# Two-layer encoder trunk: eight slots for split weights in the FFN, its last step by token block, block 0 turned at another place, first loads in another order

## What is computed

```python
for l in range(DEPTH):                      # DEPTH = 2, ALPHA = 4**0.25
    x = layer_norm(ALPHA * x + 0.5 * swiglu(x, ffn1_w13[l], ffn1_w2[l]), ...)
    h = x @ w_in[l]                         # pool channels | q | kv | rope key
    y_mix = concat([pool_mixer(...), mla_mixer(...)]) @ w_out[l]
    x = layer_norm(ALPHA * x + y_mix, ...)
    y_mem = memory_cross_attention(x, mem, mem_wq[l], mem_wkv[l], mem_wo[l])
    x = layer_norm(ALPHA * x + y_mem, ...)
    x = layer_norm(ALPHA * x + 0.5 * swiglu(x, ffn2_w13[l], ffn2_w2[l]), ...)

def swiglu(x, w13, w2):                     # d_ff = 2816
    gate, up = jnp.split(x @ w13, 2, axis=-1)
    return (jax.nn.silu(gate) * up) @ w2
```

## Time and profile before

| | us |
|---|---|
| median of 3 runs | 1175.89 (1175.66 to 1176.28) |
| the profiled execution, its time | 1177.25 |
| the profiled execution, its span | 1175.5 |
| PE busy in the span | 1123.4 |
| DVE busy | 717.6 |
| ACT busy | 511.7 |
| mean granted clock of TensorE | 0.987 |

### The profile page before, as it was taken

One profiled execution on the slowest core, in us unless ns is written; L12 is line 12 of the kernel. 1 busy time (PEld: TensorE's weight loads), 2 busy tenths in 40 slices (PEclk: granted clock), 3 DMA queues, 4 the chain that ended last, 5 costly groups with the idle time before them and its releaser, 6 DMA issues.

```text
span 1175.5 us, 16505 instructions
## 1 busy us (share of the span) xinstructions
PE 1123.4 (96%) x6020; PEld 968.4 (82%) x6020; DVE 717.6 (61%) x856; ACT 511.7 (44%) x670; POOL 106.1 (9%) x116
## 2 busy tenths in 40 slices
PE   5999999999999999999999999999999998999996
PEld 4888888899899888888888888879888986888884
DVE  3655555878766765555585555567768757555555
ACT  3544444346355254444444444434553524444440
POOL 5800000150100100000010000001401000000001
PEclk9999999999999999999999999999899998999998
DMA  8655666434482486666556665544335527665650
GB/s 257 208 185 181 194 192 196 140 117 157 126 268 93 126 267 189 186 182 194 162 183 211 194 188 188 181 141 144 121 111 190 185 88 221 200 188 183 192 161 36
DMA packets 162802, 203.56 MB, mean 173 GB/s; under 512 B 16928, under 2 KB 144160, under 8 KB 162752
## 3 DMA queue, kind: packets, MB, share of 16 engines
q1 hardware_dynamic: 159824, 194.22, 52.9%
q0 software_dynamic: 2928, 8.66, 2.3%
HBM read 201.79 MB, written 1.05 MB: 173 GB/s over the span
## 4 chain that ended last, share of the span: by engine, by line
PE 88%; DVE 7%; POOL 1%; ACT 1%; issue 1%; DMA 1%; SPq 0%; POOLq 0%; DVEq 0%
PE ps L535 84%; PE ps L698 2%; DVE st L1261 1%; DVE x L1258 1%; POOL st L1473 1%; DVE x L1280 1%; PE ps L613 1%; DVE w_lo L1168 1%; DMA raw<-in_ffn_w 1%; DVE xT L1206 0%; POOL tmp L1535 0%; DVE x L1272 0%; PE ps L796 0%; DVE v_flat L1168 0%; DVE xT L1180 0%
## 5 line engine op out<-in xcount | busy, mean ns | idle before, releaser
L1168 DVE TENSOR_TENSOR w_lo<-raw,w_hi 128x1024 fp32r<-128x1024 f32 (+2 forms) x253 | 306.9, 1221 | 170.9 <-ACT w_hi L985 170.2
L985 ACT CAST w_hi<-raw 128x1024 fp32r<-128x1024 f32 (+2 forms) x253 | 262.6, 1046 | 230.4 <-PE ps L535 201.7
L535 PE MATMUL ps<-w_hi,xT 128*128 128x512 f32 x880 | 286.4, 396 | 10.9 <-DVE w_lo L1168 9.2
L535 PEld LDWEIGHTS ps<-w_hi,xT 128*128 128x128 f32 x880 | 167.4, 190 | 46.5 <-DVE w_lo L1168 9.9
L535 PE MATMUL ps<-w_hi,mixT 128*128 128x512 f32 x704 | 202.8, 391 | 0.2
L535 PE MATMUL ps<-v_flat,xT 128*128 128x512 f32 x660 | 181.9, 397 | 4.6 <-DVE xT L1206 4.6
L535 PE MATMUL ps<-w_lo,xT 128*128 128x512 f32 x440 | 173.1, 393 | 0.0
L985 ACT CAST v_flat<-raw 128x1024 fp32r<-128x1024 f32 (+1 forms) x113 | 118.0, 1048 | 101.0 <-PE ps L535 94.3
L535 PEld LDWEIGHTS ps<-w_hi,mixT 128*128 128x128 f32 x704 | 131.2, 188 | 28.7 <-DVE mixT L1221 1.5
L535 PEld LDWEIGHTS ps<-v_flat,xT 128*128 128x128 f32 x660 | 123.6, 190 | 30.0 <-issue 4.8
L535 PE MATMUL ps<-w_lo,mixT 128*128 128x512 f32 x352 | 112.6, 390 | 0.0
(11 more groups left out here) (155 smaller groups left out, 1355.2 us busy)
## 6 DMA issues: line engine op xcount, KB each, us to landing
raw<-in_ffn_w SPq DMA_DIRECT2D x352, 256.0 KB, 3.0
raw<-in_ffn_w SPq DMA_DIRECT2D x88, 512.0 KB, 3.5
raw<-in_mem_wkv SPq DMA_DIRECT2D x32, 512.0 KB, 4.8
raw<-in_w_out SPq DMA_DIRECT2D x16, 512.0 KB, 3.8
raw<-in_mem_wq SPq DMA_DIRECT2D x16, 512.0 KB, 5.6
raw<-in_mem_wo SPq DMA_DIRECT2D x16, 512.0 KB, 4.5
gb<-in_ln_g POOLq DMA_DIRECT2D x8, 512.0 KB, 4.4
gb<-in_ln_b POOLq DMA_DIRECT2D x8, 512.0 KB, 5.3
```

The source lines that it names most:

```text
L535: return nc.tensor.matmul(dst, stand, move, start=start, stop=stop, skip_group_check=True)
L985: nc.scalar.copy(slot_hi[slot[n]][:, 0:size], raw[:, n % RAW, 0:size]).then_inc(hi_done, 1)
L1168: nc.vector.tensor_tensor(slot_lo[slot[n]][:, s], raw[:, n % RAW, s], slot_hi[slot[n]][:, s].bitcast(F32), ALU.subtract).then_inc(lo_done, 1)
```

## The change

- **Slots.** SLOTS goes from 6 to 8. The two new slots lie in `qT`, the queries' tile. They are not used for units from `win` up to `wo`, and the first units in them after that have `free_after` at `mscore, l, 1`. STEPS goes from 2 to 4.
- **The FFN's last step.** `up_end` does block 0 and then block 1, and gate, multiply, transposes and splits of that step go by block. The rows of all four last units for block 1 come after `y, e, 0` (before: of three).
- **Turning block 0.** In norms 1, 2, 5 and 6, PE turns it inside the tail, after four of the six units of the second half, and DVE's part stands ahead of the last statistics of block 1. In norms 0, 3 and 4, PE turns it between the two units of the fill.
- **The start.** x block 1 is loaded after unit 1. The constants and the memory are loaded after unit 7. The first FFN begins with units 0 and 1 for block 0 and then turns block 1. The memory is turned after `up(1)`. POOL's angles wait for `hidden, 0, 1`.

```diff
-SLOTS = 6
+SLOTS = 8
-STEPS = 2
+STEPS = 4
-    ROWS_TAIL, FFN_TAIL = 6, 4
+    ROWS_TAIL, FFN_TAIL, TURN_AFTER = 6, 4, 4
...
     def plan_rows(name, e, begun=0):
         plan.section(name, [UNIT_] * (KT - ROWS_TAIL - begun) + [[("y", e, 0)], [("half y", e)]]
-                     + [UNIT_] * (ROWS_TAIL - 1) + [["U", ("y", e, 1)]])
+                     + [UNIT_] * TURN_AFTER + turned(4 + 2 * e) + [UNIT_] * (ROWS_TAIL - 1 - TURN_AFTER)
+                     + [["U", ("y", e, 1)]])
...
+            if plan["win", l]["units"] <= n < plan["wo", l]["units"]:
+                usable.remove(6)
+                usable.remove(7)
...
-            if k >= 4 and latest[k] < plan["wout", l]["units"] <= n:
+            if k in (4, 5) and latest[k] < plan["wout", l]["units"] <= n:
                 after = done["item", plan["pv", l, PAIRS - 1]["items"]]
+            if k > 5 and latest[k] < plan["wo", l]["units"] <= n:
+                after = done["mscore", l, TB - 1]
...
+    free_after[plan["ffn", 0, 0]["units"] + 7 + SLOTS] = done["turned", 3, HALVES - 1]
...
+        slot_hi += [q_flat[:, 2 * k * UNIT:(2 * k + 1) * UNIT] for k in range(2)]
+        slot_lo += [q_flat[:, (2 * k + 1) * UNIT:(2 * k + 2) * UNIT] for k in range(2)]
...
-            for b in range(TB):
+            def load_x(b):
                 sp.dma_start(x[:, b, :], a["x"][0, b * P:(b + 1) * P, :]).then_inc(x_landed[b], 16)
+
+            load_x(0)
...
-                        if n == 2:
+                        if n == 1:
+                            load_x(1)
+                        if n == 2 * RAW - 1:
                             sp.dma_start(cst[:, P:C_ALL], consts[:, P:C_ALL]).then_inc(consts_landed, 16)
-                        if n == RAW - 1:
                             sp.dma_start(tmp[:, :].rearrange("p (b d) -> p b d", b=TB),
...
             def norm(e, l, place):
 
-                turn(4 + 2 * e, x[:, 0, :], 0, e)
-                fill(l, place)
+                if e % 4 in (0, 3):
+                    fill(l, place, lambda: turn(4 + 2 * e, x[:, 0, :], 0, e))
+                else:
+                    fill(l, place)
...
+                def up_first():
+
+                    order = [(0, 0), (1, 0), (0, 1), (1, 1), (2, 0), (2, 1), (3, 0), (3, 1)]
+                    take_bank(m + 1)
+                    for i, (j, b) in enumerate(order):
+                        if i == 2:
+                            pe.wait_ge(x_landed[1], 16)
+                            turn(1, x[:, 1, :], 1)
...
+                def up_end():
+
+                    s = FS - 1
+                    for b in range(TB):
+                        take_bank(m + 2 * s + b)
+                        for j in range(4):
+                            if b == 0:
+                                unit_split(ffn_units(u, s)[0] + j)
+                            n, last = up_block(s, j, b)
+                            if b == 0 and j == 1:
+                                turn_hidden(s - 1)
...
-                up_begin()
+                if e == 0:
+                    up_first()
+                else:
+                    up_begin()
+                up(1)
                 if e == 0:
                     pe.wait_ge(mem_landed, 16)
                     for b in range(TB):
                         turn(2 + b, tmp[:, b * D:(b + 1) * D], b)
-                up(1)
-                if e == 0:
                     for b in range(TB):
                         pe.wait_ge(turned_lo[b], turned_lo_value(3, 1))
                 down(0)
...
+                up_end()
+                rest = [down_unit(s, t) for s in (FS - 2, FS - 1) for t in range(2)]
+                for b in range(TB):
+                    pe.wait_ge(rows_ready, hidden_value(f + FS - 1, b))
+                    reach(turn_hidden_block(FS - 1, b), ("hidden", e, FS - 1, b))
+                    pe.wait_ge(bank_free, m + 2 * FS - 2 + b)
+                    for n, act in rest[2 * b:2 * b + 2]:
+                        unit_split(n)
+                        last = row_block(n, act, 0, False, n == rest[-1][0])
...
-            ahead_to(3)
+            ahead_to(2)
             turn(1, xT, 1)
...
                 if place is not None:
                     ahead_to(plan.units_by[done["y", e, 1] - 1] + 2)
+                    if e % 4 in (1, 2):
+                        turn(4 + 2 * e, xT, 0)
                 half_statistics(1, 1, ("y", e, 1))
                 variance(1)
                 center(1)
-                if place is not None:
+                if e % 4 in (0, 3) and place is not None:
                     turn(4 + 2 * e, xT, 0)
...
+            pool.wait_ge(pe_done, done["hidden", 0, 1])
             rope_angles()
```

More of the change, by code:

```diff
@@ L160, in trunk, with plan_fill @@
     UI, ITEM, UNIT_ = ["U", "I"], ["I"], ["U"]
-    def plan_fill(l, place):
+    def plan_fill(l, place, between=()):
+        assert len(FILL[l, place]) == 1 or not between
         for part in FILL[l, place]:
-            plan.section(("kv", *part), [UNIT_, UI])
+            plan.section(("kv", *part), [UNIT_, *between, UI])
             plan.n["items"] += freed_by_fill(l, place) - 1
@@ L181, in plan_norm @@
     def plan_norm(e, l, place):
-        plan_turn(4 + 2 * e)
-        plan_fill(l, place)
+        if e % 4 in (0, 3):
+            plan_fill(l, place, turned(4 + 2 * e))
+        else:
+            plan_fill(l, place)
         if e % 4 < 2:
@@ L193, in plan_ffn @@
         assert plan.n["items"] % 2 == 0
[L194 to L198, removed]
+        if e == 0:
+            marks = turned(1) + [UNIT_] * 3 + [["U", "I", "I"]]
+        else:
+            marks = turned(second_turn(e)) + [ITEM] + [UNIT_] * 3 + [UI]
+        for s in range(1, FS - 1):
+            marks += [UNIT_] * 2 + [[("hidden", e, s - 1)]] + [UNIT_, ["U", "I", "I"]]
+            marks += turned(2) + turned(3) if e == 0 and s == 1 else []
+            marks += [UNIT_] * 2
+        plan.section(("ffn", l, w), marks + [[("hidden", e, FS - 2)], ITEM] + [UNIT_] * 3 + [UI]
+                     + [[("hidden", e, FS - 1, b)] for b in range(TB)] + [[("y", e, 0)], [("half y", e)]]
+                     + [UNIT_] * 3 + [["U", ("y", e, 1)]])
     plan_turn(0)
@@ L571, in column_pair @@
                     reach(last, ("unit", n + half), *([("item", m)] if half else []))
+                    if between is not None and half == 0:
+                        between()
             def row_block(n, act, b, first, last_unit, halves=range(2)):
@@ L615, in turn, with fill @@
                     reach(last, ("turned", job, c))
-            def fill(l, place):
+            def fill(l, place, between=None):
                 for l, i in FILL[l, place]:
@@ L623, in fill @@
                     if i < 4:
-                        column_pair(m, u, memT)
+                        column_pair(m, u, memT, between=between)
                         continue
@@ L1040, in ffn @@
                 gate(1)
+                if e == 0:
+                    for b in range(TB):
+                        turn(2 + b, memT, b)
                 first = loop_first(l, w)
@@ L1057, in ffn @@
                 round_hidden(FS - 2)
+                ahead(("item", m + 2 * FS - 2))
+                gate(FS - 1, b=0)
                 ahead(("item", m + 2 * FS - 1))
-                gate(FS - 1)
-                round_hidden(FS - 1)
+                gate(FS - 1, b=1)
+                for b in range(TB):
+                    round_hidden(FS - 1, b=b)
             def norm(e, l, place):
@@ L1245, in ffn @@
                 split_hidden(FS - 2)
+                ahead(("item", m + 2 * FS - 2))
+                multiply(FS - 1, b=0)
                 ahead(("item", m + 2 * FS - 1))
-                multiply(FS - 1)
-                split_hidden(FS - 1)
+                multiply(FS - 1, b=1)
+                for b in range(TB):
+                    split_hidden(FS - 1, b=b)
             def norm(e, l=None, place=None):
```

99 lines of the change are left out of this document (52 added, 47 removed).

## The result

The changed kernel takes 1199.24 us (median; 1197.68 to 1201.31) against 1175.92 for the kernel before beside it: ratio 1.0199, 95% interval 1.0181 to 1.0217. It is slower by 2%. The profiled execution has a span of 1198.3 us against 1175.5, so the trace has to explain +22.8.

What follows compares the result with a forecast made beforehand. PE, busy 96% of the span, was taken as the bound, leaving some 50 us. Terms -9.65 + 2.1 - 1.1 - 1.4 + 17.3 + 11.5 + 4.6 gave +23.3, cut to +22: 1198 us, range 1180 to 1209.

Steps and rivals of the forecast that it cites:

- Rival 1: Whole kernel: faster, 1161 us, as extra slots only allow earlier splits and hold up no gate or maximum; 7%.
- rivals 2 and 3: Rival 2: only the memory stage pays, 1178.5 us, 10%; rival 3: only first gates and start pay, 1181 us, 7%.
- norm 2: Memory stage to FFN: two splits move ahead of block 0's completion and its turn comes in, -1.1 us.
- Start, +4.6: First FFN's beginning: earlier first product, but late gate, memory transposes, wait at down(0) and slow clock; bounds +1 to +7 us.
- the queue of loads counted from unit 2's split: Start: from 20.6 us, SP loads unit 6 (+3.7), unit 7 (+5.1), constants, memory (+8.7), units 8 to 10 (+12.9).
- Memory stage, +17.3: Memory attention: splits into new slots delay block 1's maxima, +6.0 us in layer 0, +9.55 and clock +1.7 in layer 1.
- First gates, +11.5: First gates of FFN 2, 3 and 4: splits through unit 10 stand ahead, +6.1, +2.5, and +2.0 with +0.9 for clock.
- norm 6, -1.4: Memory stage to FFN 4: PE starts 4.5 us earlier but waits 3.65 for the third unit; net -1.4 to -3.2.
- Tails, -9.65: FFN ends and following norms: by-block work saves 2.0 us each at norms 0 and 4, 1.7 at 7, 3.95 at 3.
- Norms 1 and 5, +2.1: Attention to memory stage: DVE's moved turn delays scaling 0.6 us at each; the clock may fall once; bounds +1 to +4.
- The one us that it took off the sum: Whole sum: +23.3 cut to +22, as half-speed stretches partly fall on time in which PE would wait anyway.
- The rule weighed: By the skill's rule more slots shrink gaps, and none of the +28.8 us of memory stage and first gates comes.

Runs made afterwards that it cites:

- two edits: Changed kernel with units 9 and 10 split behind each first gate: 1189.92 us; separately, changed kernel with the new slots unused until behind wo: 1185.93 us.
- The third: Changed kernel with the constants and the memory loaded behind unit 3 again instead of behind unit 7: 1194.91 us, ratio 1.0154.
- three edits: Changed kernel with units 9 and 10 behind the first gate, new slots unused until behind wo, and memory loaded behind unit 3, together: 1168.95 us, ratio 0.9941.
- the best version: Three edits, plus memory transposed before the second step, block 0 turned later in norms 1 and 5, one more unit split early in norm 6: 1157.62 us.
- the changed kernel with the old tail: Changed kernel with both blocks' last gate, product, transposes and rounding in one instruction each, as in the kernel before: 1211.45 us, ratio 1.0296.
- the edit there: Kernel with the three edits, with the memory's transposes moved back ahead of the second step's products: 1161.88 us, ratio 0.9869.

## Why the prediction was right, and where it was off

The forecast was 1198 in a range of 1180 to 1209, with 0.89 on slower; 1199.24 came. Its mechanism, splits that `ahead` moves in front of a gate and of the maxima, was shown by two edits that change only where those splits stand: they gave 10.7 and 14.1 us, and each took away the waits that it was aimed at, but for 4.36 us at the start. The third, the memory's load in SP's queue, gave 5.3. Rival 1 (splits end in time) and rivals 2 and 3 (only one of the two places pays) fall with those: each place pays by itself.

The differences by place, above, mix a wait with the slow clock behind it, which often falls into the next segment. For the comparison I take the tails and norm 2 at their forecast values, as the trace bears out the tails' size (below), and put what a segment has over to the slow stretch seen in it: 1.7 us behind 52.64, 1.4 behind 372.87, 1.8 behind 438.23 and behind 634.72, 1.7 behind 963.35.

- **Start, +4.6: too small.** (Its own terms add up to 4.4.) It is 7.0 + 1.7 = +8.7. The first product came at 11.14 (11.2 forecast), PE was through at 31.65 (31.9), and the wait behind the memory's transposes was 2.23 (2.3). But the hidden block was there at 39.81 and not at 37.2, so PE waited 8.16 and not 5.3, and both falls of the clock came. The failed step is the queue of loads counted from unit 2's split. SP issued unit 6 at 19.68, 0.9 earlier than the 20.6 of the count, and still units 7 and 8 came late. ACT's rows:

```profile
27.00 1.05 ACT L1054 CAST qT<-raw 128x1024 fp32r<-128x1024 f32 x1 [2.40 <-DMA raw<-in_ffn_w]
33.42 1.04 ACT L1054 CAST w_hi<-raw 128x1024 fp32r<-128x1024 f32 x1 [5.38 <-DMA raw<-in_ffn_w]
```

  The count lets unit 7 land at 25.7 and unit 8 at 30.7. It took 1.4 us for each 512 KB, the rate of 366 GB/s; the DMA engines moved 141 GB/s from 20 to 22 us, 263 from 22 to 24 and 279 from 24 to 26. The run with the earlier load shows that this queue is the cause: the wait fell to 2.39.
- **Memory stage, +17.3: 1.8 too large.** Layer 0: a wait of 4.2 us was forecast and 4.00 came, 4.0 + 1.4 = +5.4 (+6.0). Layer 1: five splits, as listed, moved the maxima by 8.39 us and not by 9.55; 8.4 + 1.7 = +10.1 (+11.2). The term that was mis-sized is the fifth split's load: it was put at 4.5 us, the median of the page, and landed 3.4 us after its issue at 949.35.
- **First gates, +11.5, and norm 6, -1.4: right as a sum.** Waits of 4.3, 2.5 and 2.0 us were forecast for FFN 2, 3 and 4; 3.47, 2.32 and 2.30 were found, and 3.46 for the third unit of FFN 4 (3.65). With the clock FFN 2 is 3.65 + 1.8 = +5.4 (+6.1) and FFN 3 2.3 + 1.8 = +4.1. There the forecast had +2.5 and no fall of the clock, and 0.57 stood from 636 to 640 us. FFN 4 and norm 6 are 2.5 - 1.7 = +0.8 (the forecast's terms with norm 6 give +1.5). Together 10.3 against 10.1. The -1.4 for norm 6 isn't derived in the prediction: 4.5 us earlier and 3.65 of wait leave -0.85.
- **Tails, -9.65 with norms 0, 3, 4 and 7: right.** T came 211.65 - 205.50 = 6.15 us after the last `up` product, as worked out; the end is 1.65 shorter (1.7). Norm 3 takes 17.99 us, from 596.98 (the first transposes of the tail) to 614.97 (block 0 of the FFN); 18.0 was forecast. Taken back as a whole the tail costs 8.2 to 11.4 by the ratios, of which the clock's falls elsewhere are more than half.
- **Norms 1 and 5, +2.1: 3.1 too large as a segment.** The 0.6 at norm 1 came (+0.63), but as a later gap and not as a longer one. PE's gap was to grow to 2.4 us, and it is 1.77 at both norms before and after. In layer 1 a slow stretch of the attention, which the kernel before has (0.53 and 0.62 from 844 to 852 us), was missing in the changed one, and the segment came out at -1.6. The experiments bear out the two 0.6, not a price of the clock.

The errors are +4.1, -1.8, +0.2 and -3.1: they cancel to -0.6, which is why 23.3 met 22.8. The likeliest time was hit to 1.2 us with single terms off by up to 4; that closeness is luck. The places, the list of the splits and most of the waits are the prediction's merit. The one us that it took off the sum isn't borne out, as the medians are 23.3 apart.

**The rule weighed.** The prediction set against a rule of the Trainium skill (Trainium Kernel Development and Optimization, Best Practices), that gaps can come from too little SBUF, that the loops have no gap with six slots. For the changed kernel the row was right, and more slots made more gaps. But once the bursts are out, the two slots win 8 to 9 us at the norms, which the forecast hadn't put down as theirs: with six, PE waits 2.3 us at the starts of FFN 2 and FFN 3. There the Trainium skill's rule was nearer than the prediction made it.

What stays open is how the slow clock divides over the places: the rows show the stretches, but the shares of 1.4 to 1.8 us above are argued, not measured. Also open is what decides whether the clock falls behind a given gap. The argument has one trace of each kernel, so differences of 1 to 3 us between two of them can be such falls.

## What to carry to other kernels

More buffers for prepared operands are not free where the preparation is placed greedily: each new buffer moves work in front of whatever short step stands next in the same engine's queue, and a step on which another engine waits must be ahead of it. So give a look-ahead its own limit at such steps, and don't let the number of buffers set it; here that and an earlier load, three edits of a line or two each, turned a loss of 23 us into a gain of 7. A part that costs more than it brings can hide other parts that are worth having: split a mixed change before judging it.

## What the runs showed of the hardware

- The same gap of 1.77 us stands ahead of PE's first products behind norm 1 in all fourteen traces. The clock fell behind it in ten of them (0.57 in the changed kernel) and stayed at 1.00 in four. At norm 5 the same gap was followed by a fall in one trace of fourteen.
- With the same 6020 instructions PE was busy for 1116.0 us in the best version and for 1136.5 in the changed kernel with the old tail. Their mean granted clocks were 0.996 and 0.972.
- The memory's landing took 8.2 us in the changed kernel and 9.4 in the one before, for the same 1 MB. What mattered was not that but what stood behind it: the three units that the changed order wants ahead of the gate.
- Three edits gave 30.1 us one by one and 30.3 together (within 6 or 7 us), though two of them work on the same wait. The wait behind the memory's transposes grew from 2.23 to 5.12 us, and the edit there brought 7 us where 2 to 3 was expected.
